# Sample attention of a hybrid decoder step: loads, gate and copies moved to other places in the order

## The reference

```python
# per sample member: 8 query heads in 2 groups, head dim 64
k_c, v_c = compress_kv(past rows)                      # 127 compressed keys and values
o_cmp, p_cmp = dense_attend(q, k_c, v_c)               # attention over compressed keys
idx, valid = select_blocks(p_cmp, ...)                 # 16 best of 33 blocks, by summed p_cmp
o_slc = slc_attend(q_rot, gathered blocks, idx, ...)   # selected keys (2048 past rows, paged)
o_win = win_sample(q_rot, kv_new, cache_kv_win, ...)   # window of 512 rows
o_nsa = gates[0]*o_cmp + gates[1]*o_slc + gates[2]*o_win
o_mem = mem_attend(mq, cache_kv_mem)                   # 4 heads of 128 over 256 rows
# then, for prompt and samples together
yb = einsum('bsnc,ncd->bsnd', [o_nsa, o_ml, o_mem], w_branch)
x  = x + (sigmoid(gate_raw) * yb).sum(2) @ w_out       # gate_raw = norm(x) @ w_in[:, gates]
x  = x + ffn(norm(x))
```

## Time and profile before

| | |
|---|---|
| median of 3 runs | 2583.96 us (2579.82 to 2584.76) |
| profiled execution, its own time | 2569.68 us |
| span of the profiled execution | 2568.1 us |
| mean granted TensorE clock | 0.965 of full |
| TensorE busy | 2389.3 us (93%) |
| VectorE busy | 1216.1 us (47%) |
| ScalarE busy | 813.6 us (32%) |
| GpSimd busy | 321.0 us (13%) |
| DMA moved | 156.77 MB, 61 GB/s |

### The profile page before, as it was taken

One profiled execution on the slowest core, in us unless ns is written; L12 is line 12 of the kernel. 1 busy time (PEld: TensorE's weight loads), 2 busy tenths in 40 slices (PEclk: granted clock), 3 DMA queues, 4 the chain that ended last, 5 costly groups with the idle time before them and its releaser, 6 DMA issues. The chain is left out here.

```text
span 2568.1 us, 40403 instructions
## 1 busy us (share of the span) xinstructions
PE 2389.3 (93%) x15386; PEld 2177.1 (85%) x15386; DVE 1216.1 (47%) x2160; ACT 813.6 (32%) x1779; POOL 321.0 (13%) x570
## 2 busy tenths in 40 slices
PE   6988897999877999878799999999999999999999
PEld 6977787999766889744499999987999999999997
DVE  4457665313757777466532323334434333333334
ACT  5354454444435665323321112221311111111110
POOL 1014221012204322355100000000000000000000
PEclk9998699999999999889899999999999999999999
DMA  5012432321110000277301112130211111111111
GB/s 154 21 34 67 137 109 80 98 99 34 43 35 1 1 1 1 56 183 179 98 25 50 50 42 78 50 116 1 83 50 49 34 50 50 50 39 44 50 33 66
DMA packets 216412, 156.77 MB, mean 61 GB/s; under 512 B 76338, under 2 KB 197349, under 8 KB 216164
## 3 DMA queue, kind: packets, MB, share of 16 engines
q1 hardware_dynamic: 186708, 121.96, 16.8%
q0 software_dynamic: 8160, 19.08, 2.8%
q10 hardware_dynamic: 21360, 13.22, 1.7%
HBM read 142.76 MB, written 15.59 MB: 62 GB/s over the span
## 5 line engine op out<-in xcount | busy, mean ns | idle before, releaser
L177 PE MATMUL ps<-brT_r,ff_wih 128*128 128x344 f32 x1008 | 322.0, 319 | 0.0
L179 PE MATMUL ps<-brT_r,ff_wi_r 128*128 128x344 f32 x1008 | 321.6, 319 | 0.0
L178 PE MATMUL ps<-xnT_r,ff_wih 128*128 128x344 f32 x1008 | 321.3, 319 | 0.0
L3765 ACT ACTIVATE ff_sa<-ps 128x344 f32<-128x344 f32 x66 | 30.3, 459 | 563.5 <-PE ps L179 563.5
L177 PE MATMUL ps<-x_r,mg_wh 128*128 128x344 f32 x576 | 185.4, 322 | 6.5 <-DVE xnT_r L165 6.5
L177 PEld LDWEIGHTS ps<-brT_r,ff_wih 128*128 128x128 f32 x1008 | 189.6, 188 | 1.0
L179 PEld LDWEIGHTS ps<-brT_r,ff_wi_r 128*128 128x128 f32 x1008 | 189.4, 188 | 0.0
L178 PEld LDWEIGHTS ps<-xnT_r,ff_wih 128*128 128x128 f32 x1008 | 189.0, 187 | 0.4
L178 PE MATMUL ps<-xnT_r,mg_wh 128*128 128x344 f32 x576 | 184.7, 321 | 0.0
L3801 DVE TENSOR_TENSOR x<-x,ps 128x512 f32<-128x512 f32 (+1 forms) x198 | 134.8, 685 | 100.9 <-PE ps L179 100.2
L179 PE MATMUL ps<-x_r,mg_w_r 128*128 128x344 f32 x552 | 176.2, 319 | 0.0
(11 more groups left out here) (618 smaller groups left out, 5871.5 us busy)
## 6 DMA issues: line engine op xcount, KB each, us to landing
ff_wi<-in_w_ffn_in SPq DMA_DIRECT2D x42, 512.0 KB, 5.2
mg_w<-in_w_in SPq DMA_DIRECT2D x23, 512.0 KB, 4.2
ff_wo<-in_w_ffn_out SPq DMA_DIRECT2D x11, 1024.0 KB, 4.9
s_pages<-in_cache_kv_slc POOLq DMA_DIRECT2D x128, 64.0 KB, 2.8
s_pages<-in_cache_kv_slc SPq DMA_DIRECT2D x128, 64.0 KB, 2.8
sc_X<-in_cache_kv_cmp SPq DMA_DIRECT2D x56, 128.0 KB
sc_X<-in_cache_kv_cmp POOLq DMA_DIRECT2D x56, 128.0 KB, 2.4
mg_w<-in_w_branch SPq DMA_DIRECT2D x23, 256.0 KB, 4.6
```

The lines of the kernel that those rows point to most:

```text
L177: nc.tensor.matmul(out, wh, xh, start=(first and k == 0), stop=False)
L178: nc.tensor.matmul(out, wh, xl, start=False, stop=False)
L179: ins = nc.tensor.matmul(out, wl, xh, start=False, stop=(last and k == n - 1))
L3765: nc.scalar.activation(sa[:, s % 2, :], ps[:, s % 2, 0:BLK], ACT.Silu).then_inc(silued, 1)
```

## The change

It does five things:

- The loads of the compressed keys and values are issued in `stage_slc_win`, by the sync engine, after the last turned query, into `x2` (both of them now); TensorE waits for them at the head of `stage_s_select`. `stage_s_prep` issues only the page-table load and does not wait; sync and GpSimd wait for it in `stage_s_select` ahead of their page loads.
- In `stage_s_select` the gate's multiply stands behind the ranking instead of ahead of it.
- In `stage_s_attend` ScalarE copies the turned probabilities of unit u-1 before the exponential of unit u.
- The 8 copies into `brT` become 4, each for two heads.
- In `stage_merge` the first operands are split in more parts by depth: weights k 0, 1 to 3, 4 to 11; x of the first block k 0, 1, 2, 3, 4 to 7; TensorE starts with k 0 and waits for each of the first four.

```diff
@@ stage_slc_win
+        last_q = max(m for m, x in enumerate(items) if x[0] == "q")
         with st.block() as block:
+            @block.sync
+            def _(sp):
+                sp.wait_ge(pturned, last_q + 1)
+                for dst, name in zip(kept_rows(M), ("kc_kept", "vc_kept")):
+                    sp.dma_start(dst, M[name]).then_inc(M["kept_in"], 16)
@@
+def kept_rows(M):
+    flat = M["x2"][:, :, :].rearrange("p t d -> p (t d)")
+    return flat[0:HD, 0:B * G * NCS], flat[:, 2048:2048 + B * G * HD]
@@ stage_s_prep
-                sp.dma_start(A["pt"][:, :], ...).then_inc(loaded, 16)
-                sp.dma_start(A["kcT"].rearrange("p n q -> p (n q)"), M["kc_kept"]).then_inc(loaded, 16)
-                sp.dma_start(A["vc"][:, :, :, :].rearrange("p b g d -> p (b g d)"), M["vc_kept"]).then_inc(loaded, 16)
-                sp.wait_ge(loaded, 48)
+                sp.dma_start(A["pt"][:, :], ...).then_inc(A["pt_in"], 16)
@@ stage_s_select
                 load_mem(sp, M["I"]["cache_kv_mem"], A["rows0"], 0, A["in_mem"][0])
+                sp.wait_ge(A["pt_in"], 16)
                 load_kinds(sp, ...)
@@
+                pool.wait_ge(A["pt_in"], 16)
                 load_kinds(pool, ...)
@@
+                pe.wait_ge(M["kept_in"], 32)
                 for b in range(B):
@@
-                dve.wait_ge(attended, 1)
-                nc.vector.tensor_tensor(oacc[:, :, :], ..., bc(gT[:, 0, :], 2, P), ALU.mult)
                 dve.wait_ge(attended, 2)
@@
                 nc.vector.tensor_scalar(imp[:, :], cnt[:, :], 15.5, -BIG, ALU.is_ge, ALU.mult).then_inc(ranked, 1)
+                nc.vector.tensor_tensor(oacc[:, :, :], ..., bc(gT[:, 0, :], 2, P), ALU.mult)
                 dve.wait_ge(spread, 1)
@@ stage_s_attend
-                    softmax(u)
+
                     if u >= 1:
                         keep_p(u - 1)
+                    softmax(u)
@@
-                for h in range(H):
-                    lo, g = (h % 2) * HD, h // HPG
-                    src = ps[g * HD:(g + 1) * HD, 0, 0:B * H].rearrange("p (b h) -> p b h", h=H)[:, :, h]
-                    nc.vector.tensor_copy(brT[lo:lo + HD, h // 2, S:T], src)
+                for g in range(G):
+                    rows = ps[g * HD:(g + 1) * HD, 0, 0:B * H].rearrange("p (b a q) -> p a q b", a=H // 2, q=2)
+                    for q in range(2):
+                        nc.vector.tensor_copy(brT[q * HD:(q + 1) * HD, 2 * g:2 * g + 2, S:T], rows[:, 2 * g:2 * g + 2, q, :])
@@ stage_merge
+    W_FIRST = ((0, 1), (1, 4), (4, 12))
+    X_FIRST = ((0, 1), (1, 2), (2, 3), (3, 4), (4, 8))
+    x_pieces = lambda b: ((0, 4), (4, 8)) if b else X_FIRST
@@ TensorE, step 0
-                    products(nc, ps[:, s % 4, 0:BLK], terms[:4], last=False)
+                    if s == 0:
+                        for k in range(4):
+                            pe.wait_ge(w_low, 1 if k == 0 else 2)
+                            pe.wait_ge(x_low, k + 1)
+                            products(nc, ps[:, 0, 0:BLK], terms[k:k + 1], first=(k == 0), last=False)
+                    else:
+                        products(nc, ps[:, s % 4, 0:BLK], terms[:4], last=False)
@@ ScalarE (VectorE in the same order)
-                split_first(slice(0, 4))
+                split_first(slice(*W_FIRST[0]))
                 for b in range(NB3):
-                    for k in (0, 4):
-                        high(nc, xh[:, k:k + 4, tok(b)], xnT[:, k:k + 4, tok(b)]).then_inc(x_high, 1)
-                        if b == 0 and k == 0:
+                    for lo_, hi_ in x_pieces(b):
+                        high(nc, xh[:, lo_:hi_, tok(b)], xnT[:, lo_:hi_, tok(b)]).then_inc(x_high, 1)
+                        if b == 0 and lo_ == 0:
+                            split_first(slice(*W_FIRST[1]))
+                        if b == 0 and lo_ == 3:
                             act.wait_ge(M["mg_in"][1], 16)
-                            split_first(slice(4, 12))
+                            split_first(slice(*W_FIRST[2]))
                     split_b(0, b)
```

More of the change, by code:

```diff
@@ L205, in build @@
         M["cw_high"] = nc.alloc_semaphore("cw_high")
+        M["kept_in"] = nc.alloc_semaphore("kept_in")
         M["spilled"], M["tok_in"], M["tok_in1"], M["tok_high"] = (
@@ L2377, in stage_s_prep @@
         sem = st.sem
-        turned, kept, loaded = (sem(n) for n in ("turned", "kept", "loaded"))
+        turned, kept = (sem(n) for n in ("turned", "kept"))
         chain = Chain(sem("step"))
@@ L2382, in _ @@
             def _(sp):
-                sp.dma_start(A["pt"][:, :], I["page_table"].rearrange("b n -> (b n)").unsqueeze(0)).then_inc(loaded, 16)
-                sp.dma_start(A["kcT"].rearrange("p n q -> p (n q)"), M["kc_kept"]).then_inc(loaded, 16)
-                sp.dma_start(A["vc"][:, :, :, :].rearrange("p b g d -> p (b g d)"), M["vc_kept"]).then_inc(loaded, 16)
-                sp.wait_ge(loaded, 48)
+                sp.dma_start(A["pt"][:, :], I["page_table"].rearrange("b n -> (b n)").unsqueeze(0)).then_inc(A["pt_in"], 16)
             @block.tensor
@@ L2849, in _ @@
                 nc.vector.tensor_scalar(imp[:, :], cnt[:, :], 15.5, -BIG, ALU.is_ge, ALU.mult).then_inc(ranked, 1)
+                nc.vector.tensor_tensor(oacc[:, :, :],
+                                        ps[0:H, 4:6, :].rearrange("p k (b d) -> p (k b) d", d=P),
+                                        bc(gT[:, 0, :], 2, P), ALU.mult)
                 dve.wait_ge(spread, 1)
@@ L3194, in stage_samples @@
         A["rows0"] = st.sb("rows", [P, 2, 2048])[:, :, :]
+        A["pt_in"] = st.sem("pt_in")
         for n in ("in_win", "in_mem"):
@@ L3200, in stage_samples @@
         with Stage(nc, "s2") as s2:
-            flat = M["x2"][:, :, :].rearrange("p t d -> p (t d)")
-            A["kcT"] = flat[0:HD, 0:B * G * NCS].rearrange("p (n q) -> p n q", q=NCS)
-            A["vc"] = s2.sb("vc", [P, B, G, HD])
+            kc, vc = kept_rows(M)
+            A["kcT"] = kc.rearrange("p (n q) -> p n q", q=NCS)
+            A["vc"] = vc.rearrange("p (b g d) -> p b g d", b=B, g=G)
             stage_s_prep(M, A)
@@ L3294, in _ @@
                     n, j = loads[l]
[L3295 to L3298, removed]
+                    if b == 0 and l:
+                        pe.wait_ge(w_low, l + 3)
+                    if l == 0 and b:
+                        pe.wait_ge(x_low, x_count(b) + 1)
                     if s >= 4:
@@ L3302, in _ @@
                     terms = [(wk(k), (xh[:, k, tok(b)], xnR[:, k, tok(b)])) for k in range(KT)]
-                    products(nc, ps[:, s % 4, 0:BLK], terms[:4], last=False)
+                    if s == 0:
[5 more added lines that the diff above has]
+                        products(nc, ps[:, s % 4, 0:BLK], terms[:4], last=False)
                     if l == 0:
-                        pe.wait_ge(x_low, 2 * b + 2)
-                        pe.wait_ge(w_low, 2)
+                        pe.wait_ge(x_low, x_count(b) + 2 if b else 5)
+                        pe.wait_ge(w_low, 3)
                     products(nc, ps[:, s % 4, 0:BLK], terms[4:], first=False)
@@ L3356, in split_w @@
                 def split_w(l):
-                    dve.wait_ge(w_high, l + 2)
+                    dve.wait_ge(w_high, l + 3)
                     low(nc, wl[:, l % 2, :, :], w[:, l % 2, :, :], wh[:, l % 2, :, :]).then_inc(w_low, 1)
@@ L3371, in split_b @@
                     low(nc, brR[:, 4 * n:4 * n + 4, tok(b)], brT[:, 4 * n:4 * n + 4, tok(b)], bh[:, :, tok(b)]).then_inc(b_low, 1)
-                split_first(0, slice(0, 4))
+                split_first(0, slice(*W_FIRST[0]))
                 for b in range(NB3):
-                    for k in (0, 4):
-                        dve.wait_ge(x_high, 2 * b + k // 4 + 1)
-                        low(nc, xnR[:, k:k + 4, tok(b)], xnT[:, k:k + 4, tok(b)], xh[:, k:k + 4, tok(b)]
+                    for n, (lo_, hi_) in enumerate(x_pieces(b)):
+                        dve.wait_ge(x_high, n + 1 + (x_count(b) if b else 0))
+                        low(nc, xnR[:, lo_:hi_, tok(b)], xnT[:, lo_:hi_, tok(b)], xh[:, lo_:hi_, tok(b)]
                             ).then_inc(x_low, 1)
-                        if b == 0 and k == 0:
-                            split_first(1, slice(4, 12))
+                        if b == 0 and lo_ == 0:
+                            split_first(1, slice(*W_FIRST[1]))
+                        if b == 0 and lo_ == 3:
+                            split_first(2, slice(*W_FIRST[2]))
                     split_b(0, b)
```

4 lines of the change are left out of this document (1 added, 3 removed).

## The result

The changed kernel takes 2555.72 us (median of 4 runs, 2553.45 to 2558.1), the kernel before 2581.89 (4 runs, 2577.26 to 2584.76): a ratio of 0.9906, 95% interval 0.9883 to 0.9928. That is 26.2 us by the medians and 24 by the ratio, where 18.7 were forecast; the median lies 2.8 us under the low end of the range. The profiled execution of after took 2553.88 us, with a span of 2552.3 at a mean granted clock of 0.966.

A forecast was written before the change was run, and what follows sets the result against it. TensorE, busy nearly all the span, was taken to bound the kernel, so microseconds won before 1286.2 us count whole. 3.5 + 0 + 12.4 + 1.5 + 0.7 + 0.6 = 18.7 us, from 2583.96 to 2565.3 us; range 2558.5 to 2574.

The forecast's parts named there:

- Part 4: Attention: without the wait no drop to half clock, which cost 3 us once; half taken, 1.5 us, bounds -3 and 3.
- Part 1: Preparing: compressed keys and values loaded ahead, so VectorE's last copy ends the stage; 3.5 us, bounds 2.9 and 3.8.
- (b): Rival: preparing gives nothing, as another engine's end lies under the DMA wait; 2568.8 us, chance 0.12 together with (d).
- (d): Rival: loads start late and the first ranking products wait; at worst 2568.8 us, chance 0.12 together with (b).
- Part 2: Ranking: gate multiply moved behind it shortens VectorE's chain, but the sync queue ends the stage; 0 us, bounds 0 and 1.2.
- Part 3: Attention: turned probabilities copied ahead of the exponential shorten TensorE's wait before the mem values; 12.4 us, bounds 6 and 14.1.
- it would go straight from the one to the other: Attention: TensorE passes from the window's score products to the mem values without the 2.13 us idleness.
- rival (a): The wait changes hands: TensorE waits at the next turn, the clock drop stays; 4.8 us won, 2579.2 us, chance 0.08.
- Part 5: End of attention: four copies for eight, where VectorE works alone and ends the stage; 0.7 us, bounds 0 and 1.
- Part 6: Merge: operands split in more parts by depth let TensorE start at 1.45 us instead of 3.64; 0.6 us.
- the three cases: Merge: full clock comes at 7.05, 9.2 or 11.9 us into the stage: 1.3 won, 0.4 won or 0.9 lost.
- Rival (c): Slower: the new order puts a half-clock stretch into each member's attention cycle, 3 us each; 2590.8 us, chance 0.04.

The follow-up runs named there:

- e10: Kernel before with only the gate's multiply moved behind the ranking: 2575.52 us (12 runs), ratio 1.0000 to the kernel before.
- e2: The changed kernel again, no edit: 2555.94 us (6 runs), ratio 0.9910 to the kernel before.
- e7: Changed kernel with VectorE's reciprocal and gate factor computed early, ahead of the score copies: 2550.02 us (6 runs), ratio 0.9901 to the kernel before.
- e8: Kernel before with only the merge's finer parts by depth: 2576.34 us (12 runs), ratio 0.9999 to the kernel before.
- e11: Changed kernel with VectorE's reciprocal and gate factor computed early, same kernel as e7, on another chip: 2551.47 us (6 runs), ratio 0.9898.
- e6: Changed kernel with the exponential put back ahead of the copy of turned probabilities: 2568.53 us (12 runs), ratio 0.9964 to the kernel before.
- e12: The changed kernel again, no edit, on the same chip as e11: 2555.6 us (6 runs), ratio 0.9917 to the kernel before.
- e9: Kernel before, order unchanged, with three useless TensorE products in each of seven waits ahead of the mem values: 2568.44 us (12 runs), ratio 0.9970.

## Why the prediction was off

The forecast said faster, and it was; the size was wrong. The step that failed is the size of Part 4: what the half-clock stretches behind the recurring wait cost a median execution. It was put at 1.5 us from one stretch in one execution, and the runs showed 5 to 9. The same stretches made the base of the forecast uncertain, as told below.

- **Part 1** (3.5): 3.7. Ranking starts at 1074.63 after a copy that ends at 1074.15; the gap is 0.48 us, not 0.66. Rivals (b) and (d) fell: VectorE ends the stage, and no product waits for the loads.
- **Part 2** (0): 0.2 in the profile, within the stage's scatter, nothing in e10. The page issues still end the stage.
- **Part 3** (12.4): the mechanism right, its size 11.1. Six cycles win 1.47 each, not 1.85, and 2.3 come at the stage's two ends, most of it in the last member, where 1.3 were taken. The step that failed here is "it would go straight from the one to the other": before its products TensorE also waits until VectorE has added up the unit that used the bank (`used`). In before, that sum ran from 1138.71 to 1139.05, inside the wait for the copy:

```profile
1138.71 0.34 DVE L3154 SCALAR_TENSOR_TENSOR s_oacc<-ps,sa_sm,s_oacc 8x128 f32<-8x128 f32 x1
```

The view of before's waits names L3154 once, for 0.4 us, and the copy seven times, for 14.1. The sum was the next owner, and asking what else the same instruction waits for would have found it: 2.13 less 0.67 is the 1.46 that came. Of rival (a) only the heading came true: the wait changed hands, but at the same instruction and not at the next turn, and 0.67 us of it remained.
- **Part 4** (1.5): 5 to 9 us, and here lies the miss. "As six like waits passed without one, executions differ in it. I take half" priced one stretch of one execution at half. The profiles with the waits as they were show none to three, at 3.08 us each (e10's first, a shorter one, 1.60), 1.5 of them or 4.4 us on average, and the median run has more half-clock time (191 to 196 us) than that first profile (180). The sum was set against a median 14.3 us above the profiled execution without asking whether that distance was made of the very stretches that the change removes: part of it was. The bound of 3 us for "one drop more" was too narrow by the same step.
- **The base.** The 2583.96 us are the median of three runs of a kernel whose runs scatter over 20. With a fourth it is 2581.89, and 23 to 29 runs on each of three chips give 2576.06 to 2578.61. From these the 18.7 us would have led to 2557.4 to 2559.9, 2 to 4 above the changed kernel's 2555.6 to 2555.94. So of the 9.6 us between the forecast of 2565.3 and the median that came, 5 to 8 lie in the base and 2 to 4 in the win; the clocks of those first runs aren't on record, so how far half-clock stretches raised them stays open.
- **Part 5** (0.7): 1.41 to 0.73, 0.7.
- **Part 6** (0.6): 1.9 in after, e2, e7, e8 and e11, 0.3 in e6 and e12. The order is as forecast (first product 1.42 for 1.45, second part at 6.15 for 6.3, pause 0.99 for 1.3); the clock rose earlier, about 5 us into the stage, than any of the three cases assumed (7.05, 9.2, 11.9), or, in e12, at 10. Old and new parts both vary by the clock; their averages differ by 1.3. The Trainium skill (Perfetto Trace Analysis, section Optimizing Scalar/DVE Operations) also says that breaking up instructions can let work complete sooner where ScalarE or VectorE isn't saturated but causes bubbles on another engine; the trace agrees on the bubble, 1.42 us for 3.64, though ScalarE was busy for the whole of it. Of the 0.37 us that its overhead figure would cost nothing shows: VectorE ends rows 4 to 7 at 6.09 us, where it ended them at 6.16 before.
- **Rival (c)**, half clock in each cycle, did not come: the new order has it in none ahead of the last member.

By order alone 17.2 us were forecast and 17.6 came. That the sum fits so well is luck: Part 3 was too high by 1.3 and Part 6 too low by as much. The rest of the missing win is the clock.

## What to carry to other kernels

A wait that recurs in TensorE's stream can cost twice, once as idleness and once as products at half clock behind it; count the half-clock stretches over several executions, and where the runs of a kernel scatter more than usual, suspect them. When a wait goes, look at every semaphore the waiting instruction has, not just at the one the profile names. Where a wait can't be removed, a few useless products in it, measured to be shorter than the hole, may pay. And a forecast in absolute time needs a base of many runs where they scatter.

## What was not expected of the hardware

Behind idle stretches of 2.13 us, one in each 20.73 us, the granted clock fell to 0.50 in some cycles and not in others of the same execution, and in other cycles of the next one: 9 times of 42. With 0.32, 0.57 or 0.67 us in their place it did not fall once before the last member. The Trainium skill (TensorE: Matmul & The Clock Gate, section A second HAM failure mode: psum-queue depth-cycling) describes a kernel whose short, frequent idle times between groups of products make the clock swing and cost throughput; the traces agree, with the price of 3.08 us for a stretch. On a single core the runs of the kernel before scatter over 19 to 21 us; with three products in each of the seven waits (e9) they scatter over 3. The clock's rise moves as well: for the same products of the merge it came within 4 us of the first, ahead of the pause of 0.99 us, in one execution (after), and 8.7 us behind it, with a pause of 0.91 between, in another (e12).
